# Rotary pairs of the first block laid side by side, and sixteen rotation products replaced by VectorE shuffles

## The reference, cut to what matters

```
ATT_HEADS = 8;  ATT_QK_DIM = 64;  SEQ = 256;  D_MODEL = 1024

def apply_rope(t, cos, sin):                 # t: (..., 64), float32
    t1, t2 = jnp.split(tf, 2, axis=-1)       # first 32 and last 32 dimensions
    return jnp.concatenate([t1 * cos - t2 * sin, t2 * cos + t1 * sin], axis=-1)

proj = h @ w_in                              # all projections of a layer
q = apply_rope(q_in.reshape(B, L, 8, 2, 64), cos, sin)
k = apply_rope(k_in.reshape(B, L, 8, 2, 64), cos, sin)
s = jnp.einsum('bhmqd,bhmkd->bhmqk', q, k) * scale     # only the sum over d uses q and k
```

## Time and profile before

| | before |
|---|---|
| median of three timed runs | 2478.65 us (2476.24 to 2480.4) |
| the profiled execution's own time | 2478.64 us |
| its span in the trace | 2476.8 us |
| TensorE busy | 2408.4 us (97%) |
| GpSimd busy | 1464.1 us (59%) |
| ScalarE busy | 1238.1 us (50%) |
| VectorE busy | 1172.3 us (47%) |

### The profile page before, as it was taken

One profiled execution on the slowest core, in us unless ns is written; L12 is line 12 of the kernel. 1 busy time (PEld: TensorE's weight loads), 2 busy tenths in 40 slices (PEclk: granted clock), 3 DMA queues, 4 the chain that ended last, 5 costly groups with the idle time before them and its releaser, 6 DMA issues.

```text
span 2476.8 us, 45867 instructions
## 1 busy us (share of the span) xinstructions
PE 2408.4 (97%) x18496; PEld 2121.4 (86%) x18496; DVE 1172.3 (47%) x2144; ACT 1238.1 (50%) x2133; POOL 1464.1 (59%) x853
## 2 busy tenths in 40 slices
PE   7999999999999999999999999999999999999998
PEld 7998988998999888888677877778888878999998
DVE  8897655443978655446446323231001035445144
ACT  6458654465447764455545413443323346545553
POOL 5875847557976756456342435645565546554970
PEclk9999999999999999999999999999999999999999
DMA  6544344454544453355321113232222233235554
GB/s 246 187 161 163 137 171 154 154 196 180 187 171 155 155 186 136 138 209 187 136 75 45 64 56 107 85 115 90 102 85 102 85 119 122 101 139 190 185 186 153
DMA packets 50614, 347.80 MB, mean 140 GB/s; under 512 B 5360, under 2 KB 8688, under 8 KB 8944
## 3 DMA queue, kind: packets, MB, share of 16 engines
q1 hardware_dynamic: 47840, 340.24, 37.5%
q10 hardware_dynamic: 2576, 4.72, 0.6%
HBM read 343.89 MB, written 1.05 MB: 139 GB/s over the span
## 4 chain that ended last, share of the span: by engine, by line
PE 85%; DVE 5%; ACT 5%; issue 2%; POOL 2%; DMA 1%; ACTq 0%; DVEq 0%; SPq 0%; POOLq 0%
PE pg L1966 23%; PE pg L1967 22%; PE pg L1968 22%; PE ps L2245 2%; ACT ring_hi L795 2%; PE ps L2461 1%; POOL ring_lo L666 1%; DMA ring<-in_w_stream_dram 1%; PE ps L2442 1%; PE ps L2137 1%; PE ps L2530 1%; PE ps L2523 1%; PE ps L2112 1%; PE pg L1990 1%; PE ps L2450 1%
## 5 line engine op out<-in xcount | busy, mean ns | idle before, releaser
L666 POOL TENSOR_TENSOR ring_lo<-ring,ring_hi 128x1024 fp32r<-128x1024 f32 (+3 forms) x502 | 1171.8, 2349 | 660.8 <-ACT ring_hi L795 660.2
L1966 PE MATMUL pg<-HH,ring_hi 128*128 128x256 f32 (+1 forms) x3264 | 1034.4, 317 | 12.9 <-POOL ring_lo L666 10.2
L1967 PE MATMUL pg<-HH,ring_lo 128*128 128x256 f32 (+1 forms) x3264 | 989.7, 303 | 0.0
L1968 PE MATMUL pg<-HL,ring_hi 128*128 128x256 f32 (+1 forms) x3008 | 917.1, 305 | 0.0
L1966 PEld LDWEIGHTS pg<-HH,ring_hi 128*128 128x128 f32 x3264 | 616.0, 189 | 71.5 <-issue 31.5
L1967 PEld LDWEIGHTS pg<-HH,ring_lo 128*128 128x128 f32 x3264 | 616.3, 189 | 41.0 <-issue 14.1
L1968 PEld LDWEIGHTS pg<-HL,ring_hi 128*128 128x128 f32 x3008 | 567.7, 189 | 28.1
L795 ACT ACTIVATE ring_hi<-ring 128x1024 fp32r<-128x1024 f32 (+3 forms) x572 | 564.0, 1003 | 42.0 <-DMA ring<-in_w_stream_dram 40.6
L805 ACT ACTIVATE take<-pg 128x256 f32<-128x256 f32 (+1 forms) x242 | 103.8, 429 | 419.5 <-PE pg L1968 407.0
L1968 PE MATMUL pg<-big_r,ring_hi 128*128 128x256 f32 (+1 forms) x928 | 299.4, 323 | 0.0
L1966 PE MATMUL pg<-big_r,ring_hi 128*128 128x256 f32 (+1 forms) x752 | 246.3, 328 | 3.9 <-DVE ring_lo L1642 2.7
(11 more groups left out here) (358 smaller groups left out, 3183.0 us busy)
## 6 DMA issues: line engine op xcount, KB each, us to landing
ring<-in_w_stream_dram SPq DMA_DIRECT2D x320, 1024.0 KB, 4.8
hn<-in_consts_dram ACTq DMA_DIRECT2D x2, 1024.0 KB, 5.7
cst<-in_consts_dram SPq DMA_DIRECT2D x1, 1408.0 KB, 19.9
prm<-in_params_dram SPq DMA_DIRECT2D x1, 1110.0 KB, 9.4
X<-in_xT_dram SPq DMA_DIRECT2D x1, 1024.0 KB, 5.8
X<-in_ctxT_dram ACTq DMA_DIRECT2D x1, 1024.0 KB, 7.8
out_dram<-H ACTq DMA_DIRECT2D x4, 256.0 KB, 2.2
cst<-in_consts_dram SPq DMA_DIRECT2D x1, 768.0 KB, 17.1
```

What stands on the lines that cost most here:

```text
L666: pool.tensor_tensor(ring_lo[:, slot, cols], ring[:, slot, cols], ring_hi[:, place * P:(place + n) * P].bitcast(F32), SUB).then_inc(sem(LO ...
L1966: first = pe.matmul(out, a[0], b[0], start=start, stop=False)
L1967: pe.matmul(out, a[1], b[0], start=False, stop=False)
L1968: return first, pe.matmul(out, a[0], b[1], start=False, stop=stop)
```

## The change

The weight columns of the first block's `qk` chunks are permuted on the host within each group of 64: dimension d and d + 32 now come out on neighbouring partitions. The rotated copy then needs only a swap of neighbours, and the sign goes into the sine table through the scale of its Sin activation. The frequencies `inv1` are repeated to match. The first block's rope becomes the second block's: VectorE shuffles `QK` into `ps`, and the 16 TensorE products, with their semaphore, are gone. Each rope now waits for the ScalarE copies of its two `qk` chunks instead. TensorE no longer waits for the last `qk` copy and the angle table after the second `v` part; it keeps the wait for the constant tables there, in layer 0. The 128 columns that `rot1` had are kept as unused room behind `tab1`, and a new column `turn1` (the signs) moves the constants behind it by one column.

```
             def rope(i, qk, cos, sin):
-                dve.wait_ge(sem("rot"), i + 1)
+                turned = ps[:, 2 + i % 2, :].rearrange("p (a b) -> p a b", a=2)
+                link(dve.stream_shuffle(turned, qk, PARTNERS))
                 dve.tensor_tensor(cut(at_buf, 0, 2, T), qk, rep(cos, 2), MUL).then_inc(sem("rope_cos"), 1)
-                turned = ps[:, 2 + i % 2, :].rearrange("p (a b) -> p a b", a=2)
                 link(dve.tensor_tensor(turned, turned, rep(sin, 2), MUL))
...
+                def rope1(jj):
+                    dve.wait_ge(sem("drained"), DRAINED["qk", l, 2 * jj + 1])
+                    rope(8 * l + jj, QK[:, 2 * jj:2 * jj + 2, :], tab[:, 0, :], tab[:, 1, :])
...
-            def rot(i, table, qk):
-                if i >= 2:
-                    pe.wait_ge(sem("rope"), i - 1)
-                pe.matmul(ps[:, 2 + i % 2, :], table, qk, start=True, stop=True).then_inc(sem("rot"), 1)
...
-                    if part == 1:
-                        pe.wait_ge(sem("drained"), DRAINED["qk", l, 15])
-                        if l == 0:
-                            pe.wait_ge(sem("rope_table"), 1)
-                            pe.wait_ge(sem("tables"), 32)
-                    if part in (1, 2):
-                        rot1(2 * part - 2)
-                        rot1(2 * part - 1)
+                    if part == 1 and l == 0:
+                        pe.wait_ge(sem("tables"), 32)
                 for i in range(24):
-                    if i in (1, 2, 5, 6):
-                        rot1(ROPES_V + (1, 2, 5, 6).index(i))
...
+    sides = np.arange(P).reshape(P // QK_DIM, 2, half).transpose(0, 2, 1).reshape(-1)
+        if name == "qk":
+            return [t[:, sides] for t in w1[l](AQ + i * P)]
...
-                        act.activation(tab[:, 1, :], POSF, ACT.Sin)
+                        act.activation(tab[:, 1, :], POSF, ACT.Sin, scale=C("turn1"))
```

More of the change, by code:

```diff
@@ L59, in constants @@
     c["levels"] = np.concatenate(lv, 1)
-    rot1 = np.zeros((P, P))
-    for d in range(P):
-        if d % QK_DIM < QK_DIM // 2:
-            rot1[d + QK_DIM // 2, d] = -1.0
-        else:
-            rot1[d - QK_DIM // 2, d] = 1.0
-    c["rot1"] = rot1
-    c["tab1"] = np.zeros((P, 2 * T))
+    c["tab1"] = np.zeros((P, 2 * T + P))
     t = np.arange(T)
@@ L75, in constants @@
     inv1 = 10000.0 ** (-np.arange(0, QK_DIM, 2, dtype=f) / QK_DIM)
-    c["inv1"] = np.tile(inv1, 4)[:, None]
+    c["inv1"] = np.tile(np.repeat(inv1, 2), 2)[:, None]
+    c["turn1"] = np.where(i % 2, 1.0, -1.0)[:, None]
     tt = np.linspace(0.0, 1.0, T)[:, None]
@@ L103, in constants @@
     return c
-CONST_W = {"until": P, "later": P, "causal1": T, "levels": 7 * P, "rot1": P, "tab1": 2 * T,
-           "ident": P, "ones": P, "eps6": 1, "eps5": 1, "half_pi": 1, "lam_init": DEPTH, "inv1": 1,
+CONST_W = {"until": P, "later": P, "causal1": T, "levels": 7 * P, "tab1": 2 * T + P,
+           "ident": P, "ones": P, "eps6": 1, "eps5": 1, "half_pi": 1, "lam_init": DEPTH, "inv1": 1, "turn1": 1,
            "cos2": T, "sin2": T, "zT": T, "dft_fwd": NT * N_FFT, "idft": 4 * T,
@@ L494, in build @@
         ident, ones, eps6, eps5 = C("ident"), C("ones"), C("eps6"), C("eps5")
-        tab = C("tab1").rearrange("p (a b) -> p a b", a=2)
+        tab = C("tab1", 0, 2 * T).rearrange("p (a b) -> p a b", a=2)
         assert CONST_AT["ident"] >= 4 * HY
@@ L1712, in _ @@
                         dve.wait_ge(sem("rope_table"), 1)
-                rope1 = lambda jj: rope(8 * l + jj, QK[:, 2 * jj:2 * jj + 2, :], tab[:, 0, :], tab[:, 1, :])
+                def rope1(jj):
+                    dve.wait_ge(sem("drained"), DRAINED["qk", l, 2 * jj + 1])
+                    rope(8 * l + jj, QK[:, 2 * jj:2 * jj + 2, :], tab[:, 0, :], tab[:, 1, :])
                 for jj in range(ROPES_V):
@@ L1834, in rope2 @@
                     dve.wait_ge(sem("hn_done"), HN_BASE2[l] + (1, 2, 0, 3)[jj])
-                dve.wait_ge(sem("rope"), i)
-                turned = ps[:, 2 + i % 2, :].rearrange("p (a b) -> p a b", a=2)
-                link(dve.stream_shuffle(turned, qk, PARTNERS))
-                dve.tensor_tensor(cut(at_buf, 0, 2, T), qk, rep(C("cos2"), 2), MUL).then_inc(sem("rope_cos"), 1)
-                link(dve.tensor_tensor(turned, turned, rep(C("sin2"), 2), MUL))
-                dve.wait_ge(sem("rope_cos"), i + 1)
-                dve.tensor_tensor(qk, cut(at_buf, 0, 2, T), turned, ADD).then_inc(sem("rope"), 1)
+                rope(i, qk, C("cos2"), C("sin2"))
             for l in range(DEPTH):
@@ L2374, in _ @@
                     chunk("qk", l, i, KD, hx, T)
-                rot1 = lambda jj: rot(8 * l + jj, C("rot1"), QK[:, 2 * jj:2 * jj + 2, :])
                 for part in range(4):
@@ L2570, in lay_out @@
              "a_out": "w_attn_out", "d_out": "w_dn_out", "oa": "w_o_attn_2", "oh": "w_o_hyena_2"}
-    single1 = {"qk": AQ, "dn": DQ, "cz": CZ, "az": AZ, "dz": DZ}
+    single1 = {"dn": DQ, "cz": CZ, "az": AZ, "dz": DZ}
+    half = QK_DIM // 2
+    sides = np.arange(P).reshape(P // QK_DIM, 2, half).transpose(0, 2, 1).reshape(-1)
     single2 = {"q2": Q2, "k2": K2, "hy2": HY2}
```

## The result

| | before | after |
|---|---|---|
| median of 14 runs | 2478.53 us (2475.61 to 2480.4) | 2484.42 us (2480.93 to 2487.82) |
| the profiled execution's own time | 2478.64 us | 2485.61 us |
| its span | 2476.8 us | 2482.5 us |

The account below looks back on a forecast made before the run. The prediction took TensorE as the bound, with VectorE becoming it in the `dn` stage. From 2478.64 us it took 2.0 us gain per layer and added 1.6 us clock loss per layer: 2477.9 us, range 2470 to 2484.

Parts of the forecast that it names:

- What bounds: Whole kernel: TensorE is busy 97% of the span; in the `dn` stage VectorE runs level, 34.79 of 35 us.
- the removed products: TensorE: the rotation products taken out are worth 6.8 us per layer, 13.7 us in all.
- the new wait in the v stage: Third and fourth `v` parts: TensorE waits for GpSimd's `ring_lo` pieces, 1.1 us together, ends 0.7 and 1.8.
- VectorE's chain: `dn` stage: four uncovered shuffles take 2.9 us, so TensorE waits 0.8 us ahead of `dn` 6, 2.9 ahead of `dn` 10.
- that rival: `dn` stage: shuffles wait for GpSimd, 1.90 us each, 4.7 us more per layer; 2490.8 us, chance 0.04.
- The size of the gain: `dn` stage: TensorE starts `dn` 10 some 2.0 us earlier per layer, not 6.8.
- The cosine products: Ropes in the `dn` stage: first longer, about 2.6 us, second short, others as before, sum kept as it was.
- The clock: Behind `dn` 10: TensorE's clock probably drops once in each layer, costing 1.6 us each time.
- VectorE gets ahead again and the 2.0 us stay: After `dn` 10: TensorE needs 5.7 us for two chunks, VectorE 4.7 us, so the 2.0 us gain is kept.
- touch nothing that TensorE waits for: Moved constants, 64 KB less in the first table transfer, and the sign as a Sin scale: costed at nothing.
- if TensorE's 2.0 us are lost again behind `dn` 10: Behind `dn` 10: a listed sign that the prediction is wrong, given without a price.
- Rival C: `dn` stage: VectorE's chain through four ropes outgrows the gain; 2484.4 us (chance 0.08) or 2490.8 us (0.04).

Follow-up runs that it names:

- no_shuf: The changed kernel without the first block's eight shuffles per layer, the rotated copy left out: 2473.34 us (0.9983).
- before_shuf: The kernel before, all products kept, plus a shuffle with unused output in each first-block rope, 16 in all: 2492.75 us (1.0063).
- after_again: The changed kernel, unaltered, run and profiled a second time: 2483.92 us (1.0024).
- swap: The changed kernel with VectorE's filter argument moved ahead of the small modulation instructions at the end of layer 1: 2481.04 us (1.0015).
- after_64: The changed kernel with 65 empty TensorE instructions added, ahead of the first norm and of layer 1's first chunk: 2478.16 us (1.0003).
- after_256: The changed kernel with 256 empty TensorE instructions ahead of the first norm, as a control: 2506.80 us, 2482.4 us without the delayed start.
- before_192: The kernel before with 192 empty TensorE instructions ahead of the first norm: 2499.41 us, 2482.1 us less the later start.
- half_rot: The changed kernel with ropes 4 to 7 of each layer rotated by TensorE products again, ropes 0 to 3 by shuffle: 2476.56 us (0.9995).
- half_rot_swap: half_rot with the filter argument also ahead of the modulation parts at the end of layer 1: 2476.42 us (0.9996).
- ropes8: The changed kernel with all eight ropes of a layer ahead of the `dn` stage, last-`conv31` taps moved there in exchange: 2475.11 us (0.9987).

## Why the prediction was wrong

- **What bounds, the removed products, the new wait in the v stage:** right in kind. The wait was 1.37 us in layer 0 and 1.36 in layer 1, where I took 1.1 with an end at 1.8. It stood at the third part alone, where 0.7 to 0.8 was forecast: GpSimd's pair of pieces took 5.31 us (121.01 to 126.32) and not 4.74.
- **VectorE's chain:** right in its mechanism, with a shuffle of 0.69 us. The waits were 1.03 and 0.69 us ahead of `dn` 6 (0.8 forecast) and 2.77 and 2.78 ahead of `dn` 10 (2.9). None of the 16 shuffles was held up by GpSimd. (The price of that rival, 4 x 1.2, is 4.8 and not 4.7, which moves nothing.) no_shuf and before_shuf show from both sides that the shuffles make them.
- **The size of the gain:** mis-sized in layer 0. `dn` 10 starts at 170.58, and 171.3 before: 0.7 us earlier, 0.9 with the later start of the program taken off, not 2.0. Two terms of the chain failed. The second `sconv` instruction, which follows the copy of `dn` 1, runs at 144.35, so this copy ends at that time and not at 143.5: TensorE arrives 0.9 us later than worked out, of which the longer wait in the `v` stage is 0.3 and the start of the program 0.2; the rest I can't place. And VectorE needs 22.18 us from rope 4 to `sconv` 6 (146.31 to 168.49), against 18.80 before (149.86 to 168.66): 3.4 us for the four shuffles, where I had 2.9; one of them starts after 0.36 us of idle that no wait explains. The cosine products came as forecast, one at 2.56 us, the second short at 0.69, and a sum of 6.4 us against 6.6 before. In layer 1, from 612 us to the row behind the stage, the change gained 1.3 us, and no low clock followed its wait of 2.78 us in this profile.
- **The clock:** right in kind. It dropped behind `dn` 10 in layer 0 of all five profiles with this `dn` stage (after, after_again, swap, after_64, after_256), and in layer 1 of three. Over 100 to 1192 us, the stretches of low clock sum to a loss of 6.8 us (after) and 8.5 (after_again), against 3.4 and 1.7 in the two profiles of the kernel before. I had 3.2 us more in the sum, and these are 3.4 to 6.8. What came on top lies at the layer ends.
- **The step that failed** is "VectorE gets ahead again and the 2.0 us stay", with its fellow, the list of things that "touch nothing that TensorE waits for". The prediction named the outcome ("if TensorE's 2.0 us are lost again behind `dn` 10"), but gave it no price and no mechanism. Missing was a part of the removal: 65 instructions fewer in TensorE's stream. That moved a packet into the load that feeds the end of layer 1, ScalarE waited 3.66 us for it in place of 2.09, and 4.4 us went there; 2.6 us more went at the end of layer 0, where the same cause is less sure. With them put back the changed kernel takes 2478.16 us, 0.5 us above the kernel before of its session, where 0.7 us below was forecast. So the mechanism of the forecast is the one that acts where it looked, and 5.4 to 6.3 us come from a resource that it didn't look at: the DMA engines that TensorE's instruction packets share with the weight loads. That 2478.16 is so near the forecast 2477.9 is partly luck: by after_64's profile the change loses 0.8 us up to the end of the `dn` stage of layer 0 and 0.4 us in that of layer 1, where a gain of 0.4 us each was forecast.
- **Rival C** forecast 2484.4 us by longer cosine products and a wait of over 4 us. The time was met, but not the mechanism.

**What stays open.** At the end of layer 0 the match is weaker. Packets 0.4 to 0.8 us behind the issue go with waits of 1.17 to 1.78 us, those 0.9 to 1.7 us behind it with 1.91 to 2.41 us, but one profile had 3.98 us at 0.6 us. In before_192 the packet came 4.0 us behind it, with 1.08 us. That a DMA engine serves the packet in the middle of the load and the load ends with the last of 16 engines is argued from 0.98 us for the packet and the delay of 1.2 us in the median, not shown engine by engine. Why the packet near layer 1's end stands 1.1 us behind the issue in one profile of the changed kernel and 2.7 us in the other is open too. And 1.6 us at the very start come and go between profiles of otherwise equal starts, half_rot and half_rot_swap among them: the wait of 2.2 us near 41 is there in all, the low clock behind it in 12 of 18. That is part of the difference between the profiles of after and after_64, though hardly of that between the medians.

## What to carry to other kernels

A removed instruction also moves the fetches of its engine's stream, for the rest of the program. Where weights are loaded just in time, look in the DMA view for instruction packets that fall into a load on which the chain hangs, and before giving up on a change, put back the count of instructions with empty ones where the engine idles anyway. Moving work from one engine to another that is as busy brings nothing by itself. Here it paid 2.6 us with the ropes moved out of the stage where both are full (ropes8), and 10 us with the swap and the 65 empty instructions as well. Small VectorE instructions with two SBUF inputs don't belong ahead of anything urgent while GpSimd works through long pieces.

## What the runs showed of the hardware

- A 16 KB instruction packet took 0.98 us of one DMA engine. A 1 MB weight load with one 1.0 to 2.7 us behind its issue made ScalarE wait 3.5 to 4.1 us, in eight profiles; with the packet ahead of the issue it was 2.1 to 2.7 us, in the ten others.
- A satisfied wait isn't free on TensorE: 192 empty instructions put its first product at 27.62 us and 256 at 34.83 us, 0.11 us for each of the 64 between them. Two waits went into one instruction: 512 of them moved the packets by one whole piece.
- VectorE instructions of 0.2 us took up to 2.46 us while GpSimd's pieces of about 2.4 us ran, four times in a row. The Trainium skill, "SBUF — State Buffer", section "SBUF: two separate sides", has the port pair locked for a whole instruction; the trace agrees, and shows that the lock is lost anew for each instruction of a row.
- At the end of layer 0 the wait for `ring_lo` was 1.08 to 1.78 us in ten profiles, and the clock stayed at 2.4 GHz behind it in all ten. In eight it was 1.91 to 3.98 us, and the clock fell to 1.2 GHz in all eight, at about 1.7 us each. A transfer half a microsecond later thus cost over 2 us at this place. At other places the length of the wait did not decide alone: behind 2.2 us near 41 us the clock fell in 12 of 18 profiles, and behind 2.77 us ahead of layer 1's `dn` 10 in three of five.
